# Reading a recurrent state for one chunk at a time instead of for two, in the mixer of a hybrid decoder layer

## What is computed

```python
def step(state, inp):
    qc, kc, vc, gc = inp
    b = jnp.cumsum(gc, axis=2)
    o_inter = jnp.einsum('bhck,bhkv->bhcv', qc * jnp.exp(b), state)
    ...
    o_intra = jnp.einsum('bhts,bhsv->bhtv', A, vc)
    b_last = b[:, :, -1:, :]
    new_state = (jnp.exp(b_last[:, :, 0, :])[..., None] * state
                 + jnp.einsum('bhsk,bhsv->bhkv', kc * jnp.exp(b_last - b), vc))
    return new_state, o_inter + o_intra
```

## Time and profile before

| | us |
|---|---|
| median of 3 runs | 638.96 |
| lowest, highest | 638.18, 641.46 |
| the profiled execution, whole | 638.18 |
| its span, first to last instruction | 636.2 |
| TensorE busy | 612.7 (96%) |
| VectorE busy | 474.0 (74%) |
| ScalarE busy | 378.2 (59%) |

### The profile page before, as it was taken

How to read it: one execution, slowest core, us unless ns; L and a number is a source line. 1 busy time by engine, 2 the same in 40 slices (tenths; PEclk the granted TensorE clock), 3 DMA queues, 4 the chain that set the end, 5 groups by cost and what they waited for, 6 DMA issues and landing times.

```text
span 636.2 us, 9823 instructions
## 1 busy us (share of the span) xinstructions
PE 612.7 (96%) x3763; PEld 494.4 (78%) x3763; DVE 474.0 (74%) x549; ACT 378.2 (59%) x405; POOL 108.3 (17%) x79
## 2 busy tenths in 40 slices
PE   8999999999999999999799999999999999999991
PEld 7878788877778888888578788888888888888870
DVE  3758598884467334456699988888988898889967
ACT  4669333441116676411547877878778778887745
POOL 0003222380000000000078321111011111110010
PEclk9999999999999999999989999999999999999996
DMA  9832132224106000975579999999999999999654
GB/s 328 274 127 72 51 127 91 67 74 73 67 2 199 2 2 1 367 293 221 209 270 419 419 389 359 404 407 390 391 390 390 390 389 404 406 399 388 245 166 132
DMA packets 42558, 155.79 MB, mean 245 GB/s; under 512 B 11939, under 2 KB 12147, under 8 KB 30236
## 3 DMA queue, kind: packets, MB, share of 16 engines
q1 hardware_dynamic: 37500, 138.40, 55.6%
q0 software_dynamic: 5024, 16.92, 10.3%
HBM read 139.96 MB, written 15.34 MB: 244 GB/s over the span
## 4 chain that ended last, share of the span: by engine, by line
PE 90%; DVE 5%; issue 2%; ACT 2%; DMA 1%; DVEq 0%; SPq 0%; ACTq 0%
PE psum L636 25%; PE psum L638 24%; PE psum L637 23%; PE psum L866 3%; PE psum L1018 2%; PE psum L749 2%; PE psum L1035 1%; PE psum L645 1%; PE psum L844 1%; PE psum L857 1%; DMA cst<-in_c_main 1%; DMA misc<-x_dram,first 1%; PE psum L791 1%; PE psum L735 1%; PE psum L779 1%
## 5 line engine op out<-in xcount | busy, mean ns | idle before, releaser
L1714 DVE TENSOR_TENSOR w_lo<-ring,w_hi 128x2048 fp32r<-128x2048 f32 x95 | 217.5, 2307 | 23.3 <-ACT w_hi L1316 23.2
L636 PE MATMUL psum<-w_hi,act_hi 128*128 128x512 f32 x544 | 220.3, 405 | 2.6 <-DVE w_lo L1714 1.0
L638 PE MATMUL psum<-w_hi,act_lo 128*128 128x512 f32 x544 | 212.7, 391 | 0.0
L637 PE MATMUL psum<-w_lo,act_hi 128*128 128x512 f32 x544 | 212.4, 391 | 0.0
L1316 ACT ACTIVATE w_hi<-ring 128x2048 fp32r<-128x2048 f32 x96 | 182.1, 1916 | 24.7 <-PE psum L638 24.7
L636 PEld LDWEIGHTS psum<-w_hi,act_hi 128*128 128x128 f32 x544 | 102.4, 188 | 29.7 <-DVE w_lo L1714 6.2
L638 PEld LDWEIGHTS psum<-w_hi,act_lo 128*128 128x128 f32 x544 | 102.1, 188 | 22.1
L637 PEld LDWEIGHTS psum<-w_lo,act_hi 128*128 128x128 f32 x544 | 102.4, 188 | 18.8
L1158 ACT ACTIVATE w_hi<-ring 128x2048 fp32r<-128x2048 f32 x17 | 32.5, 1913 | 46.8 <-PE psum L638 45.5
L590 POOL DMA_INDIRECT acc_dram<-misc,slots x15 | 23.7, 1582 | 201.1 <-ACT misc L1366 191.1
L1475 DVE TENSOR_TENSOR w_lo<-ring,w_hi 128x2048 fp32r<-128x2048 f32 x17 | 39.8, 2344 | 22.1 <-ACT w_hi L1158 21.9
(11 more groups left out here) (242 smaller groups left out, 712.8 us busy)
## 6 DMA issues: line engine op xcount, KB each, us to landing
ring<-in_w_gate SPq DMA_DIRECT2D x32, 1024.0 KB, 13.9
ring<-in_w_up SPq DMA_DIRECT2D x32, 1024.0 KB, 16.3
ring<-in_w_down SPq DMA_DIRECT2D x32, 1024.0 KB, 14.9
ring<-in_w_in SPq DMA_DIRECT2D x13, 1024.0 KB, 6.1
ring<-in_w_o SPq DMA_DIRECT2D x4, 1024.0 KB, 5.5
acc_dram<-ring SPq DMA_DIRECT2D x5, 512.0 KB, 3.6
ring<-in_x SPq DMA_DIRECT2D x2, 1024.0 KB, 6.3
ring<-strip_dram SPq DMA_DIRECT2D x8, 256.0 KB, 4.9
```

What stands on the lines that cost most here:

```text
L636: pe.matmul(dst, lh, rh, start=first, stop=False, skip_group_check=True)
L637: pe.matmul(dst, lh, rl, start=False, stop=False, skip_group_check=True)
L638: return pe.matmul(dst, ll, rh, start=False, stop=last, skip_group_check=True)
L1714: dve.tensor_tensor(w_lo[:, v0 % WBUF, :], ring[:, slot, :], w_hi[:, v0 % WBUF, :].bitcast(F32), ALU.subtract).then_inc(s_lo, 1)
```

## The change

`from_states(i)`, which handled chunks 2i and 2i+1 in one batch with their matmuls in turn, becomes `from_state(c)` for one chunk. Chunk 0 no longer waits for s_state; chunk c waits for s_state to be c (before, the pair waited for 2i+1). The wait for s_rgated stays with the even chunk. In the table, the even chunks go to slots 3 and 10, and the odd ones stay at slots 5 and 13, where the pair was. Nothing else changes; lines behind 779 move up by one.

```diff
-            def from_states(i):
-
-                if i == 0:
+            def from_state(c):
+
+                rows, i = slice(64 * (c % 2), 64 * (c % 2) + 64), c // 2
+                if c == 0:
                     pe.wait_ge(s_copied, GROUPS)
                     pe.wait_ge(s_qe, 1)
                     pe.wait_ge(s_zero, 1)
-                pe.wait_ge(s_state, 2 * i + 1)
-                if i >= 2:
+                else:
+                    pe.wait_ge(s_state, c)
+                if c % 2 == 0 and i >= 2:
                     pe.wait_ge(s_rgated, i - 1)
                 for a in range(PAIRS):
-                    for c in (2 * i, 2 * i + 1):
-                        rows = slice(64 * (c % 2), 64 * (c % 2) + 64)
-                        last = pe.matmul(psum[rows, 4 + i % 2, a * P:(a + 1) * P], qe[:, a, c * CH:(c + 1) * CH],
-                                         state[:, c % 2, a, :], start=(a == 0), stop=False, skip_group_check=True)
-                        if a == PAIRS - 1:
-                            last.then_inc(s_inter, 1)
+                    last = pe.matmul(psum[rows, 4 + i % 2, a * P:(a + 1) * P], qe[:, a, c * CH:(c + 1) * CH],
+                                     state[:, c % 2, a, :], start=(a == 0), stop=False, skip_group_check=True)
+                last.then_inc(s_inter, 1)
...
+                    elif slot == 3:
+                        from_state(c0)
                     elif slot == 5:
-                        from_states(c0 // 2)
+                        from_state(c0 + 1)
...
+                    elif slot == 10:
+                        from_state(c0 + 2)
                     elif slot == 13:
-                        from_states(c0 // 2 + 1)
+                        from_state(c0 + 3)
```

## The result

The changed kernel takes 645.72 us, the kernel before 640.88 us, medians of 16 runs each. The ratio is 1.0073 with a 95% interval of 1.0049 to 1.0096: slower by 0.7%, some 4.7 us. Its profiled execution took 642.03 us, with a span of 640.2 us.

A forecast was written before the change was run, and what follows sets the result against it. TensorE was taken as the bound, holding 90% of the chain and busy 37.33 of 37.71 us. State batches 9.76 - 5.35 = +4.4 us on 638.18 give 642.6, with the three-run median 643.4; 643.0 was taken, range 641.2 to 646.2.

The forecast's parts named there:

- A batch of one chunk costs as much as one of two: Line 779 state batches: eight records in one column half take eight steps of 0.109 us, 1.22 us a batch.
- The fixed part: In each state batch on TensorE: 0.35 us for going into the split array and back.
- The first wait: First state batch: its 0.47 us goes, since chunk 0 needs no state; it is in the 5.35 us already.
- No new wait: TensorE's state batches in units 11 and 12: every needed update ends in time, chunk 1's with 0.9 us to spare.
- VectorE's earlier permissions: VectorE's 5.3 us of waits for line 779 shorten, but this is worth nothing.
- The sum: State batches of units 11 and 12: eight cost 9.76 us against 5.35 before, +4.4 us.
- All of it reaches the end: Behind the recurrence: ScalarE, VectorE and weight loads hang on TensorE's progress, so all 4.4 us count.
- the base of three runs: Starting time for the whole kernel: the median of three runs, 0.8 us above the profiled 638.18 us.
- steps slower by 40 to 50 ns: State batches: 64 steps that are 40 to 50 ns slower, setting the range's upper end of 646.2 us.
- half a batch in half the time: Rival on state batches: 0.055 us a record in either half, 0.79 us a batch, change +0.97 us; 10%.
- Weight loads standing in line: Rival on state batches: loads no longer overlap matmuls, steps up to 0.246 us, +13.2 us, 651.4; 5%.
- The delay: Rival in the expert loop: busy DMA engines hide the mixer's late end, giving about 639; 5%.

The follow-up runs named there:

- e1: Kernel before, each state batch reordered to four even-chunk matmuls, then four odd-chunk ones; a batch cost 1.71 us, first key-value record to first score 50.43 us.
- e8: Kernel before, with each state batch's eight matmuls ordered even, even, odd, odd, even, even, odd, odd; a batch cost 1.27 us.
- e2: Kernel before plus four single state-type matmuls (two records each) in the split array, at the new even batches' places; each cost 0.56 us.
- e3: Kernel before plus four single matmuls at the new even batches' places, with 128 weight columns, so on the full array; each cost 0.22 us.
- r3: Kernel before, unchanged, profiled a third time; 48.58 us from first key-value batch to first score, 439.7 us from there to the end.
- r1: Kernel before, unchanged, profiled again; 48.55 us from first key-value batch to first score, 432.1 us from there to the end.
- e6: e4 plus key-value matmuls of two chunks in turns and first state and chunk batches at slot 7; 638.23 us against 641.11 before, ratio 0.9953.
- e4: Kernel before, pairs kept, key-value batches joined and state batches put directly before chunk products in units 11 and 12; timed ratio 0.9912.

## Why the prediction was right

Forecast were 643.0 us within 641.2 to 646.2, slower; measured are 645.72. Step by step:

1. *A batch of one chunk costs as much as one of two*: 1.22 us forecast, 1.21 to 1.23 measured, with single starts 0.11 us apart. The reading that carried it, pairs of records in the earlier trace rows against single records in the earlier trace rows, holds; e1 and e8 show that it is the order of the halves that counts, at an equal number of records.
2. *The fixed part is 0.35 us*: e2 measured 0.34 to 0.35, e3 none for the full array. With it, the eight batches add up to 9.75 us (9.76 forecast).
3. *The first wait goes*: it went, 0.47 us.
4. *No new wait*: none. Chunk 1's batch stands at 161.69 (161.60 forecast), the update it needs ends at 160.78 (160.70).
5. *VectorE's earlier permissions are worth nothing*: its waits for line 779 fell by 3.4 us, TensorE's timetable didn't notice.
6. *The sum is +4.4 us*: 4.40 measured in the stretch. By parts: four more fixed parts, 4 x 0.345 = 1.4; four times the eight steps in which the other half is idle, 4 x 0.87 = 3.5; the wait, -0.5.
7. *All of it reaches the end*: the ratio gives 4.7 us (3.1 to 6.2) and agrees. Between the two profiled executions it is only 4.0 us (640.2 less 636.2), because the rest took 0.5 less; r3 against r1 shows that the rest moves by more than that on its own.

The absolute number came out 2.7 us under the measured median. That isn't the change: the base of three runs, 638.96, was low by 1.9, the median of 16 is 640.88, and I had taken 643.0 instead of 643.4. The runs of before spread from 638 to 645 us, and three runs don't show that; the gather's wait, which I didn't know of, may well be the reason, since the profiles r1 and r3 lie as far apart, but the timed runs have no traces. 640.9 + 4.4 would have been 645.3. That 645.72 still lies in the range, 0.5 us under its upper end, is luck in part: that end was drawn for steps slower by 40 to 50 ns, which didn't come, and not for a base that was too low.

The rivals: half a batch in half the time needed 0.79 us where 1.22 are measured, and e1 refutes its rate per record. Weight loads standing in line would have made steps longer than before; there are none. The first step of a batch is 0.160 us in both kernels (before, 170.52 to 170.68), all others are 0.109, and the loads are 137 ns long as in the earlier trace rows, though all eight records of a batch use the same rows and columns of the array:

```profile
L779 PEld LDWEIGHTS psum<-misc,ring x64: 132/137/137, 159.1 to 194.3; 128*64 128x64 f32 x64
L779 PE MATMUL psum<-misc,ring x64: 272/273/323, 159.1 to 194.4; 128*64 128x128 f32 x64
```

So the rule of the Trainium skill, page "TensorE: Matmul & The Clock Gate", Part 3, that a load overlaps a matmul in flight only when the row group differs, doesn't hold for these batches. The same Part 3 also names a load into a background weight buffer as one that goes ahead; these rows fit that, but no run here shows which buffer a load used.

The delay was not absorbed. The Trainium skill, page "TensorEngine Tiling (Array Packing)", Key Properties, says that different tiles can work in parallel and that a change of the tiling mode drains TensorE. The runs agree with the first (e1, e8, e6); for the second they show a price, 0.34 us (e2), and none without a change (e3), but not the draining itself.

Three numbers expected of the experiments were wrong: e4's timed ratio, which stays unexplained, e6's gain over e4, where a wait came back, and the cost of e1's batch. There I took the stream as strictly in order, and TensorE went ahead over three waiting records, at each of the three places in e1 and e8.

## What to carry to other kernels

Small matmuls that write one half of the output partitions are only half of a batch. Give them a partner for the other half, in turns or at least in short blocks, before asking whether they can be issued earlier: splitting a pair doubled its cost here, 1.22 to 2.44 us. And count the ways from full-array matmuls into the split array and back, 0.34 us each here; put split batches side by side, and let their tiles differ. An earlier permission for an engine that waits anyway was worth nothing here, while the engine that gives it was full.

## What the runs showed of the hardware that I had not expected

- TensorE takes matmuls of another tile ahead of waiting ones. With four matmuls of one half before four of the other, the second half began 0.49 us into a row of 0.87 us, with three records of the first still to start, and with blocks of two and two there were three again, twice.
- Row halves count as column halves do: 32 records of 64 columns cost 0.82 us in four quarters and 1.28 us in two (line 791, and its successor line 790).
- A change between two split modes (128x64 to 64x64) costs 0.15 us, less than the way through the full array (0.34).
- A gather late by 5 us cost more than its wait: in r3 everything from it on took 8.0 us longer for a wait of 5.1, because the granted clock stood at 0.50 from 408.5 to 415.3 us, mostly behind the wait.
